# Attention over pairs of key tiles with 64-column value stationaries, and the normalisation of the probabilities on GpSimd

## The reference

```python
# h = rmsnorm(x); z = h @ w_in, split into q, k, v, indexer, conv and gate parts
score = einsum(wi, relu(qi . ki)); score = where(admissible, score, -inf)
_, idx = top_k(score, topk)                       # 256 keys (40 for the stream)
logits = einsum('bqhgd,bqkhd->bqhgk', q, k[idx]) * HEAD_DIM ** -0.5
p = softmax(where(valid, logits, -inf))
o = einsum('bqhgk,bqkhd->bqhgd', p, v[idx])       # 8 query heads, 2 kv heads, head size 64
m = sigmoid(ga) * (o @ w_attn_out) + sigmoid(gb) * y_conv
```

## Time and profile before

| what | value |
|---|---|
| median of 3 runs | 3200.93 us (3200.27 to 3201.02) |
| the profiled execution's own time | 3198.51 us |
| its span | 3196.7 us |
| mean granted TensorE clock | 0.983 |
| TensorE, VectorE, ScalarE, GpSimd busy | 96%, 68%, 33%, 39% of the span |
| values matmuls of key tiles, L1084 | 304 instructions, 157.9 us busy |
| attention stage | about 167 us in each layer |

### The profile page before, as it was taken

The page is one execution under the profiler, slowest core; times in us unless marked ns, Lnnn a source line. Parts: engine busy times, 40 slices in busy tenths (PEclk is TensorE's granted clock), DMA queues, the critical chain, the costliest instruction groups (busy, mean ns, idle before and its releaser), DMA issues.

```text
span 3196.7 us, 54413 instructions
## 1 busy us (share of the span) xinstructions
PE 3072.6 (96%) x20484; PEld 2941.4 (92%) x20484; DVE 2173.8 (68%) x3818; ACT 1063.1 (33%) x1938; POOL 1251.2 (39%) x736
## 2 busy tenths in 40 slices
PE   5999999999999999999979999989999999999998
PEld 4999998669999999999979999976799899999998
DVE  6259998845585656774572799988446856576735
ACT  5430112750353333433244201137413433333321
POOL 2023333004637764445330233320155477644460
PEclk8999999999999999999989999989999999999999
DMA  3121224103323446754231212230133244477533
GB/s 137 54 73 40 67 94 135 34 28 123 105 99 105 145 142 212 257 191 172 99 121 60 67 47 75 93 120 27 48 119 102 91 132 144 140 248 260 177 131 109
DMA packets 164574, 369.50 MB, mean 116 GB/s; under 512 B 18528, under 2 KB 60096, under 8 KB 164416
## 3 DMA queue, kind: packets, MB, share of 16 engines
q10 hardware_dynamic: 114144, 209.45, 18.3%
q1 hardware_dynamic: 50272, 157.96, 15.4%
HBM read 261.53 MB, written 105.83 MB: 115 GB/s over the span
## 4 chain that ended last, share of the span: by engine, by line
PE 79%; DVE 11%; DMA 3%; issue 3%; ACT 2%; POOL 2%; ACTq 1%; SPq 0%; DVEq 0%; POOLq 0%
PE PS L782 25%; PE PS L1186 16%; PE PS L1251 14%; PE PS L791 8%; PE PS L865 5%; PE PS L1084 3%; PE PS L1044 2%; PE PS L1067 2%; PE PS L953 1%; PE PS L915 1%; PE PS L897 1%; DVE X L2171 1%; DVE X L2177 1%; DMA HN<-f_keep 1%; DVE HN L2126 1%
## 5 line engine op out<-in xcount | busy, mean ns | idle before, releaser
L782 PE MATMUL PS<-H,W 128*128 128x358 f32 (+1 forms) x4032 | 663.6, 327 | 0.6 <-POOL W L605 0.6
L782 PEld LDWEIGHTS PS<-H,W 128*128 128x128 f32 x4032 | 662.2, 189 | 0.7 <-POOL W L605 0.7
L603 POOL TENSOR_TENSOR W<-RAW,ones 128x1024 fp32r<-128x1024 f32 x80 | 157.4, 1968 | 880.7 <-PE PS L782 828.6
L1251 PE MATMUL PS<-FB,DW 128*128 128x268 f32 (+1 forms) x3456 | 424.4, 285 | 1.0 <-DVE FB L2741 1.0
L1251 PEld LDWEIGHTS PS<-FB,DW 128*128 128x128 f32 x3456 | 423.9, 188 | 1.4 <-POOL DW L738 1.2
L2395 DVE TENSOR_SCALAR_CACHE_REDUCE PASS<-SC,TC,CST 128x400 bf16<-128x400 f32 x372 | 356.1, 1019 | 1.7
L1186 PE MATMUL PS<-TT,WF 128*128 128x268 f32 (+1 forms) x2688 | 339.2, 285 | 0.0
L1186 PEld LDWEIGHTS PS<-TT,WF 128*128 128x128 f32 x2688 | 334.0, 188 | 0.1
L1186 PE MATMUL PS<-H,WF 128*128 128x268 f32 (+1 forms) x2016 | 259.4, 286 | 3.1 <-ACT SQ L1748 1.6
L1186 PEld LDWEIGHTS PS<-H,WF 128*128 128x128 f32 x2016 | 252.8, 189 | 4.3 <-issue 4.3
L865 PE MATMUL PS<-WQ,H 128*128 128x364 f32 (+1 forms) x1296 | 240.9, 342 | 12.2 <-POOL WQ L610 5.6
(11 more groups left out here) (256 smaller groups left out, 4943.6 us busy)
## 6 DMA issues: line engine op xcount, KB each, us to landing
RAW<-in_w_slab SPq DMA_DIRECT2D x168, 512.0 KB, 3.6
RAW<-in_w_half SPq DMA_DIRECT2D x56, 384.0 KB, 4.0
DR<-in_w_half SPq DMA_DIRECT2D x56, 384.0 KB, 3.7
FL<-f_keep ACTq DMA_DIRECT2D x18, 1072.0 KB, 10.1
FL<-f_keep ACTq DMA_DIRECT2D x18, 1056.0 KB, 10.3
f_keep<-TB ACTq DMA_DIRECT2D x48, 268.0 KB, 4.5
f_keep<-TB ACTq DMA_DIRECT2D x48, 264.0 KB, 4.4
SK<-in_w_half SPq DMA_DIRECT2D x32, 384.0 KB, 3.3
```

What stands on the lines that cost most here:

```text
L603: g_.tensor_tensor(hi, raw, one, ALU.mult).then_inc(hi_split, 1)
L782: mm = nc.tensor.matmul(PS[:, b0 + c, 0:cw], W[:, s, w, k, :], act[:, a, k, c * cw:(c + 1) * cw], start=(first and w == 0 and a == 0), sto ...
L1251: last = nc.tensor.matmul(PS[:, to + c, 0:qw], DW[s][:, w, kk - u * UNITK, :], down_act(q, a, kk, c * qw, (c + 1) * qw), start=(kk == 0 an ...
```

## The change

Pairs: from a = 2 on (t = 1 to 7), an odd key tile of 128 is worked on together with the one before it. `BATCHES` lists the steps so grouped; both tiles of a pair are transposed, then both are multiplied. The stationary has only the 64 columns of the group's kv head; even key tiles write partitions 0 to 63 of the bank, odd ones 64 to 127. The meta values have a stationary for each kv head whose second 64 columns are zero. ScalarE copies the half that does not lie where it is wanted, VectorE adds the other. `PT` has four buffers. The four rows of logits are spread over a group's batches.

Normalisation: VectorE makes only the reciprocal (`inverse`), GpSimd multiplies. GpSimd's rows stand between the split of slab pair S_MERGE / 2 = 14 and that of the next. `outputs(i - 1)` moves behind `meta_rows(i + 1)` in VectorE's order, and `o_hi_copy(i - 2)` and `o_lo_part(i - 2)` go to a group's second batch.

```diff
-        PT = at("PT", [P, 3, 512], F32, r_q + 10 * 256 * 4)
+        PT = at("PT", [P, 4, 512], F32, r_q + 10 * 256 * 4)
...
+        BATCHES = []
+        for _u, (_a, _kv, _kt) in enumerate(STEPS):
+            paired = _a >= 2 and _kt % 2 == 1 and key_tiles(ORDER[_a])[_kt][2] == P
+            if paired:
+                BATCHES[-1].append(_u)
+            else:
+                BATCHES.append([_u])
+        def place(n):
+
+            a, kv, kt = STEPS[BATCHES[n][0]]
+            mine = [us for us in BATCHES if STEPS[us[0]][0:2] == (a, kv)]
+            return NKV * a + kv, mine.index(BATCHES[n]), len(mine)
+
+        def rows_at(n):
+
+            i, b, nb = place(n)
+            return [(j, g) for j, g in ROW_UNITS if j == i + 2 and max(g, 0) * nb // GROUP == b]
...
-                split_slabs(2, S_WO // 2)
+                split_slabs(2, S_MERGE // 2 + 1)
+
+                def normalise(i, g):
+
+                    t, c, n = ORDER[i // NKV], i % 3 * GROUP + g, (l * NGRP + i) * GROUP + g + 1
+                    m, row = ROWS[t], prob(PA, i, g)[0:ROWS[t], 0:EXT[t]]
+                    g_.wait_ge(rden_made, n)
+                    g_.tensor_scalar(row, row, RDEN[0:m, c:c + 1], None, ALU.mult).then_inc(p_ready, 1)
+
+                for i in range(NGRP):
+                    for q in range(GROUP):
+                        normalise(i, q)
+
+                split_slabs(S_MERGE // 2 + 1, S_WO // 2)
...
+                    elif a >= 2:
+                        h = kt % 2
+                        nc.tensor.matmul(PS[h * HD:(h + 1) * HD, 6 + kv, 0:GROUP * m], V[0:w, vt, kv * HD:(kv + 1) * HD],
+                                         PT[0:w, u % 4, 0:GROUP * m], start=(kt < 2), stop=False).then_inc(pv_done, 1)
...
-                for u in range(NU):
-                    for j, g in rows_at(u):
+                for n, us in enumerate(BATCHES):
+                    for j, g in rows_at(n):
                         logits(j, g)
-                    if u + 1 < NU:
-                        turn_p(u + 1)
-                    values(u)
+                    if n + 1 < len(BATCHES):
+                        for u in BATCHES[n + 1]:
+                            turn_p(u)
+                    for u in us:
+                        values(u)
...
+                def o_half_copy(i):
+
+                    a, kv = divmod(i, NKV)
+                    m = ROWS[ORDER[a]]
+                    act.wait_ge(pv_done, l * NU + ENDS[i])
+                    act.wait_ge(o_lo, l * 18 + i - 1)
+                    for odd in range(2):
+                        copy(O2[odd * HD:(odd + 1) * HD, i % 2, :, 0:m], half_of(kv, 1 - odd, m)[:, :, odd, :])\
+                            .then_inc(o_half, 1)
...
+                    if part == 0 and i > 2 * NKV:
+                        o_half_copy(i - 1)
+                    if part == 1 and i > 1:
+                        o_hi_copy(i - 2)
...
-                def normalise(i, g):
+                def inverse(i, g):
...
                     dve.wait_ge(exp_done, n)
                     V_.reciprocal(RDEN[0:m, c:c + 1], DEN[0:m, c:c + 1]).then_inc(rden_made, 1)
-                    dve.wait_ge(rden_made, n)
-                    V_.tensor_scalar(row_, row_, RDEN[0:m, c:c + 1], None, ALU.mult).then_inc(p_ready, 1)
...
+                        if a >= 2:
+                            dve.wait_ge(o_half, (l * (NGRP - 2 * NKV) + i - 2 * NKV) * 2 + 2)
+                            o = PS[odd * HD:(odd + 1) * HD, 6 + kv, 0:GROUP * m].rearrange("p (g o m) -> p g o m", o=2, m=m)
+                            to = O2[odd * HD:(odd + 1) * HD, i % 2, :, 0:m]
+                            V_.tensor_tensor(to, to, o[:, :, odd, :], ALU.add).then_inc(o_made, 1)
+                            continue
...
-                        if x == 0 and kt == 0 and i:
-                            outputs(i - 1)
                         if x < len(behind):
-                            normalise(*behind[x])
+                            inverse(*behind[x])
...
-                    if kt == 0 and NKV <= i + 1 < NGRP:
+                    if part == 0 and NKV <= i + 1 < NGRP:
                         meta_rows(i + 1)
-                    if kt == min(2, n - 1) and i > 1:
+                    if part == 0 and i:
+                        outputs(i - 1)
+                    if part == 1 and i > 1:
                         o_lo_part(i - 2)
```

More of the change, by code:

```diff
@@ L340, in build @@
         RANK = at("RANK", [P, EXT[7]], F32, r_q + 10 * 256 * 4)
-        PT = at("PT", [P, 3, 512], F32, r_q + 10 * 256 * 4)
-        PTR = at("PTR", [P, 3, 512], F32R, r_q + 10 * 256 * 4)
+        PT = at("PT", [P, 4, 512], F32, r_q + 10 * 256 * 4)
+        PTR = at("PTR", [P, 4, 512], F32R, r_q + 10 * 256 * 4)
         r_f = r_q + 10 * NKV * HD * 4
@@ L348, in build @@
         MT = at("MT", [P, 2, GROUP, NST], F32R, r_f)
-        VM = at("VM", [P, NKV * HD], F32R, r_f + 2 * GROUP * NST * 4)
-        assert 2 * GROUP * NST * 4 + NKV * HD * 4 <= 10 * (256 - NKV * HD) * 4
+        VM = at("VM", [P, 1 + NKV, NKV * HD], F32R, r_f + 2 * GROUP * NST * 4)
+        assert 2 * GROUP * NST * 4 + (1 + NKV) * NKV * HD * 4 <= 10 * (256 - NKV * HD) * 4
         S0 = at("S0", [P, CW], F32, r_q + 10 * 256 * 4 + 2048)
@@ L436, in build @@
         o_made, o_hi, o_lo = sem("o_made"), sem("o_hi"), sem("o_lo")
+        o_half = sem("o_half")
         pads_zero, mask0 = sem("pads_zero"), sem("mask0")
@@ L645, in _ @@
                 g_.memset(MT[:, :, :, :].bitcast(F32), 0.0).then_inc(mt_clear, 1)
-                g_.memset(VM[:, :].bitcast(F32), 0.0).then_inc(mt_clear, 1)
+                g_.memset(VM[:, :, :].bitcast(F32), 0.0).then_inc(mt_clear, 1)
                 def split_slabs(g0, g1, other=0, before=0):
@@ L1079, in values @@
                     if w == N_META:
-                        pe.wait_ge(vm_made, (l + 1) * 3)
-                        nc.tensor.matmul(PS[:, 6 + kv, 0:GROUP * m], VM[0:NST, :], PTR[0:NST, u % 3, 0:GROUP * m],
-                                         start=False, stop=True).then_inc(pv_done, 1)
+                        pe.wait_ge(vm_made, (l + 1) * 6)
+                        nc.tensor.matmul(PS[:, 6 + kv, 0:GROUP * m], VM[0:NST, 1 + kv if a >= 2 else 0, :],
+                                         PTR[0:NST, u % 4, 0:GROUP * m], start=False, stop=True).then_inc(pv_done, 1)
+                    elif a >= 2:
+                        h = kt % 2
+                        nc.tensor.matmul(PS[h * HD:(h + 1) * HD, 6 + kv, 0:GROUP * m], V[0:w, vt, kv * HD:(kv + 1) * HD],
+                                         PT[0:w, u % 4, 0:GROUP * m], start=(kt < 2), stop=False).then_inc(pv_done, 1)
                     else:
-                        nc.tensor.matmul(PS[:, 6 + kv, 0:GROUP * m], V[0:w, vt, :], PT[0:w, u % 3, 0:GROUP * m],
+                        nc.tensor.matmul(PS[:, 6 + kv, 0:GROUP * m], V[0:w, vt, :], PT[0:w, u % 4, 0:GROUP * m],
                                          start=(kt == 0), stop=(kt == len(key_tiles(t)) - 1)).then_inc(pv_done, 1)
@@ L1584, in _, with half_of @@
                 q_load(2)
+                def half_of(kv, h, m):
+                    return PS[h * HD:(h + 1) * HD, 6 + kv, 0:GROUP * m].rearrange("p (g o m) -> p g o m", o=2, m=m)
+                def o_half_copy(i):
[6 more added lines that the diff above has]
+                            .then_inc(o_half, 1)
                 def o_hi_copy(i):
@@ L1601, in _ @@
                 behind = [(1, g) for g in range(GROUP)]
[L1602 to L1606, removed]
-                        q_load(a + 2)
[L1608 to L1614, removed]
+                for n, us in enumerate(BATCHES):
+                    i, part, _ = place(n)
+                    a, t = i // NKV, ORDER[i // NKV]
+                    m = ROWS[t]
+                    if i % NKV == 0 and part == 0 and 0 < a < 7:
+                        q_load(a + 2)
+                    for u in us:
+                        w = key_tiles(t)[STEPS[u][2]][2]
+                        act.wait_ge(turned_p, l * NU + u + 1)
+                        if u >= 4:
+                            act.wait_ge(pv_done, l * NU + u - 3)
+                        if w == N_META:
+                            copy(PTR[0:NST, u % 4, 0:GROUP * m], PS[0:NST, 4 + u % 2, 0:GROUP * m]).then_inc(pt_made, 1)
+                        else:
+                            copy(PT[0:w, u % 4, 0:GROUP * m], PS[0:w, 4 + u % 2, 0:GROUP * m]).then_inc(pt_made, 1)
@@ L1615, in _ @@
                     for j, g in behind:
                         exponent(j, g)
[L1617 to L1623, removed]
+                    behind = [(j, g) for j, g in rows_at(n) if g >= 0]
+                    if part == 0 and i > 2 * NKV:
+                        o_half_copy(i - 1)
@@ L1626, in gate_load @@
+                    if part == 1 and i > 1:
+                        o_hi_copy(i - 2)
+                o_half_copy(NGRP - 1)
+                o_hi_copy(NGRP - 2)
+                o_hi_copy(NGRP - 1)
```

(15 more changed lines are left out.)

6 lines of the change are left out of this document (3 added, 3 removed).

## The result

The changed kernel takes 3207.05 us (median, 3203.83 to 3209.71), the kernel before 3200.08. The ratio is 1.0023 with a 95% interval of 1.0016 to 1.0030: slower by about 7 us, where 3181 and a gain of 20 had been forecast. The time lies inside the stated range, close to its upper end, and on the other side of no change. By experiment 1 the pairs and their order shortened TensorE's path by more than was forecast; a new loop through GpSimd and VectorE took that back and a little more. In the first layer the attention stage goes from the first logits at 540.22 us to the first merge slab at 711.15 us, 170.9 us instead of 167.4.

A forecast was written before the change was run, and what follows sets the result against it. TensorE, busy 96% of the span, bounds the kernel. Shorter groups save 26.4 us; 1.5 us per layer each for waits and stationary changes leave 20.4, so 3198.5 becomes 3178, plus 2.4 gives 3181 us; range 3157 to 3208.

The forecast's parts named there:

- GpSimd's price: Normalising rows on GpSimd: 63 us per layer, the middle of 40 and 86, hidden below half the attention stage.
- The serial wait: VectorE's new wait for GpSimd at meta_rows: two late rows, about 1.2 us, in two-batch groups; one with more batches.
- GpSimd's wait: Rival: late rows stall VectorE some 2 us in each of the first 10 groups; 3215 us, chance 0.06.
- The pair: Two values matmuls on TensorE partly overlap: 1.29 us instead of 1.72, 0.43 saved, 27.5 us over both layers.
- three slots: Started in order, the second product's first pass runs beside the first's low pass: three 0.43 us slots; chance 0.42.
- fully side by side: Rival: a pair's two values products overlap wholly on TensorE, saving 0.86 us a pair; 3159 us, chance 0.15.
- The switch: Changing between half and full stationaries on TensorE: 0.04 us on each of 38 batches, 1.5 us per layer.
- Slower, by the switch: Rival: width changes empty TensorE's array, some 0.3 us a batch; 3221 us without overlap, chance 0.12.
- the values matmuls are on TensorE's path: In the attention stage, TensorE is full from 603 us on, so shortening values matmuls pays.
- ScalarE's half copies: Two 64x256 copies per group from t = 1 on: 0.40 us each, 10 us per layer, hidden from t = 3.
- The end of the stage hides the added copies: Two half copies add 0.8 us behind the last values, hidden by the first merge slab's convolution half.
- VectorE's relief in the early stage: VectorE loses 72 multiplications per layer, 32 us effective; early groups t = 1 and 2 put at 5.7 and 6.5 us.

The follow-up runs named there:

- experiment 1: The changed kernel with the normalising multiplication put back on VectorE right behind the reciprocal, pairs kept: 3160.28 us.
- Experiment 4: The changed kernel with GpSimd's multiplication written as a product of two tensors, the inverse broadcast along the row: 3153.05 us.
- experiments 3 and 4: The first: the changed kernel with meta_rows of a group moved to that group's own first batch, 3169.34 us; the second: see Experiment 4.
- experiment 7: The kernel of experiment 1 with every key tile a batch of its own, 64-column stationaries kept: 3228.20 us.
- experiment 6: The kernel of experiment 1 with 128-column stationaries for all values matmuls, order by pairs kept, half copies gone: 3186.78 us.

## Why the prediction was wrong, point by point

**GpSimd's price.** This is the step that failed. The operation had no row; I bounded it by a memset and by a product with a broadcast operand, and took the second for an upper bound without a reason. The form with a scalar costs 2.6 ns a column where that bound had 1.61 and the value taken lay between it and 0.84. Experiment 4 shows that this is the step on which the sign hung: with rows at the upper bound and everything else as changed, the kernel takes 3153. GpSimd's rows are 119 us per layer (152.8 and 85.2 us for both groups of rows over both layers) and not 63. The Trainium skill ("GPSIMD Engine Reference", Engine selection) puts operations with one input at about line rate on GpSimd; the trace disagrees, 2.94 us against VectorE's 0.76, and against 1.95 for the two-operand form on GpSimd itself.

**The serial wait.** `meta_rows` was named as the new wait, and the rival "GpSimd's wait" had the mechanism: late rows stall VectorE, and the masks and exponents move with it. Its place was right and its extent too small. I took two late rows of four in the small groups and one in the others. In fact the four rows run back to back and VectorE waits for the last of them in every group, because the reciprocals that let GpSimd start also stand behind the wait. I compared GpSimd's sum with the stage, while in a loop the parts add: 7.78 and 2.32 us per group of 656 columns. Price and wait together cost the changed kernel the 47 us between it and experiment 1, and either repair alone brings most of it back (experiments 3 and 4). The rival's 3215 was closer than my forecast and had the mechanism; it had been given a chance of 0.06. It counted 2 us a stall in 10 groups, and the trace has 3.6 in 16.

**The pair.** Forecast 0.43 us saved of 1.72, by three slots; the trace has 0.71, both first passes together. The order of the passes, on which the three slots rested, does not keep the second product waiting: its first pass starts 6 ns behind the first product's, and both second passes 0.48 us later. In the kernel one product stands behind the other; in which order the compiled passes were issued, no trace shows, so whether matmuls started in program order here stays open. The rival "fully side by side" was right in mechanism, but its 0.86 is not reached: the pair takes 1.01. The rest fits weight loads that start only with the pair (0.13 us each, behind 0.17 us without any), which was not tested by itself. What the prediction works out from the 2.38 times that the Trainium skill ("TensorE: Matmul & The Clock Gate", Part 3) has for three column tiles is off as well. At the same rate per tile two tiles would be 1.6 times as fast, an estimate of 0.64 us saved and not 0.86. The trace has 1.70 times.

**The switch.** Forecast 0.04 us per batch from rows with 48-column stationaries; it is 0.29 to 0.36 (experiment 7). So the "Slower, by the switch" rival had its price right (0.3), and the Trainium skill ("TensorEngine Tiling (Array Packing)", Key Properties), which has a change of tiling mode drain the array, fits these numbers, though the traces show the price and not the draining itself. The errors in the pair and in the switch nearly cancel, and that is luck. Per pair 0.71 less 0.2 behind it is 0.51, 32.6 us for 64 pairs; 12 single tiles lose 0.35 each, 4.2; that makes 28, and experiment 6 measured 26.5. Forecast for the same were 27.5 less 3.

**What held.** That the values matmuls are on TensorE's path: in experiment 1 TensorE is full from 603 us on, and its stage, put at about 148 us beforehand, took 149.1. ScalarE's half copies take 0.38 us (0.40 taken), 10.6 us per layer, and hide. The end of the stage hides the added copies; only one wait of VectorE for the gates' DMA is new there (4.4 us once, behind it TensorE goes on). VectorE's relief in the early stage did not come through, since VectorE waited instead of computing.

**The clock.** The low stretch at the first stage's start was as before (0.59 from 541 to 562 us in both); later the windows show 0.95 and 0.88 where they had 1.00. It falls behind gaps in TensorE's work, so it is a consequence of the loop and a part of the loss. The part has a bound, an estimate from windows of 10 us: from 571 to 601 and 661 to 671 us in the first layer and from 2160 to 2260 us in the second they miss 12 us of the full clock in all, so it is at most about 12 of the 47 us.

## What to carry to other kernels

When an operation moves to another engine, do not compare sums: draw the loop. If the giver waits for the result in its own instruction order before it issues what the taker needs next, both engines' times add, and the place of that wait can be worth as much as the operation's speed (38 us here by moving it, 54 by making the rows shorter). The two do not add: moved too late the wait stops TensorE instead, and with both repairs the kernel took 3170, while the right place gave 3150. A bound taken from another operation on the same engine is no bound until its form is the same. Half-width stationaries paid here only in adjacent pairs: every section of them cost about a third of a microsecond, whether a pair or a single tile, and single tiles alone made the kernel slower than before (3228).

## What the runs showed of the hardware

GpSimd multiplies a row by a scalar per partition in 2.94 us at 1040 columns, by a constant in 2.87, and as a product with the scalar broadcast along the row in 1.95; at 400 columns 1.28, 1.21 and 0.90. Two f32 products with 64-column stationaries and outputs in different PSUM halves run side by side, first passes and then second passes, though each has two passes and one product stands behind the other in the kernel: 1.01 us for two, 1.00 for one, 1.72 for two with full stationaries.
